# A three-block model on one core: the decay of the gated linear attention computed beside its product, a bias table written in eight parts, constants on another queue

## The chip, the core and the metric

One Trainium2 chip, one of its cores. The metric is the device time of one launch in microseconds. All arithmetic is fp32; the products are made of three passes over operands that are split into a high part (fp32r) and a low part.

## What is computed

Three transformer-like blocks over 512 tokens of 1024 features (528 in block 1, with 16 meta tokens). Block 1: RWKV-7 mixing and differential attention, gates, an MLP. Block 2: a gated convolution and sparse attention with a relative-position bias. Block 3: mLSTM, gated linear attention (GLA) and gated delta net, then gates and an MLP. The change touches three places of it.

```
h = rms_norm(h_res, norm_mix_w)                      # block 1, opening
p = h @ w_in ;  r,k,v,w,a,g from p, token shift       # block 1, projections
bias(h, distance) = rel_bias[bucket(distance), h]     # block 2, table of 8 x 640 values

q, k, v, gate, low = split(h3 @ w_in_3)               # block 3, GLA
log_decay = log_sigmoid(low @ w_gla_lr + b_gla) / 16
for each token t:  S = exp(log_decay[t]) * S + k[t] v[t]^T ;  o[t] = S^T q[t] / sqrt(128)
o = rms_norm_per_head(o) * silu(gate)

o_m = rms_norm_per_head(mlstm) * g_head_mlstm         # HeadNorm, block 3
```

## The kernel before, in words

Every engine has its own program and its own order, written out by hand; semaphores tie them together. A `stage` is a block of five such programs, with a barrier of all engines at its end, which also frees the stage's memory and semaphores.

*`opening`* (L1898) normalises x for block 1 and makes the tables of the bias. SP's queue brings x, `ones`, the norm weight and the first weight slab (L1922 to L1926), writes the row of 640 biases of each head 128 times to DRAM (`bias_by_distance`, called `far`, L1928: 2560 KB from 8 partitions) and a table by residue (`near`, L1930), and waits for both. ScalarE squares x, copies the rows out of PSUM, takes the root (L1962), issues the loads of twelve constants (L1964), and then rounds the eight normalised tiles to their high parts (L1967); VectorE multiplies (L1991) and makes the low parts (L1988).

*`rwkv_project`* (L569) multiplies h with 27 weight slabs of 512 KB in a ring of three (`first` and two `wbuf`). Its eight rounds each make r, k, v, decay, a and gate for two heads. SP's program of a round (L627 to L634): the three slabs of the round after next, a wait for `fac_ready` (VectorE's last operation of the round, `bonus`) and `g_out`, three stores (`factors`, `bonus`, `gate`), then the vectors of two rounds on. ScalarE (L744 to L767) in a round: two sigmoids, a square, one eviction and the high part of a slab that SP has just ordered, the gate's copy, three exponentials, the root `kn`, two more evictions and high parts. VectorE (L779 to L822) makes the factors; POOL makes the slabs' low parts (L646). The stage ends when all stores have landed.

*`chain`* (L97) is the product over a list of jobs, used throughout. A slab s is 8 k-tiles of one output tile: 24 matmuls. With ring=3, ScalarE makes the high part of slab s+2 in its step s (L249), VectorE its low part (L331), and evicts tile s (L381), which waits for the product of slab s. TensorE waits for the low part of each slab (L220). A `side` object can add operations of its own at each step, on each engine, behind the chain's (L239, L319, L449). Its matmuls go to one of the two `stat` banks. In block 3 the first `chain` makes 2 small tiles and the 16 tiles of z (q 0 to 3, k 4 to 7, v 8 to 11, gate 12 to 15) with `GateRows` (L2296) at its side: the gate rows of mLSTM and delta net, in steps 1 to 6.

*`gla`* (L2480) follows: SP loads the low-rank gate weight and bias, TensorE multiplies (L2541), VectorE adds the bias (L2692), ScalarE takes Abs, Exp and Ln, VectorE makes the log decay (L2697, L2698), its running sums `cum` in windows of 128 (L2700), the distance to the window's end in `ring[2]` (L2703), ScalarE its exponential (L2634), VectorE multiplies it into the keys (L2706), and only then can TensorE transpose these keys (L2560) and make the states (L2566, L2734 to L2736). In between the values are transposed and copied (L2550, L2632). Seven levels of scores inside a window follow; POOL makes the arguments of three of them (L2527).

*`HeadNorm`* (L1467) stands at the side of block 3's last `chain`. For head h in steps 3h to 3h+2: ScalarE squares o_m (L1492) behind its eviction, TensorE sums over the partitions (L1483), VectorE and ScalarE make the root (L1503, L1495), VectorE the reciprocal and the product (L1506, L1510).

Of the kernel before, what the change touches and what calls it, by code (L numbers as in the profile page):

```python
# [9 lines left out]
ALU = mybir.AluOpType  # L10
ACT = mybir.ActivationFunctionType
AX_X = mybir.AxisListType.X
P = 128
# [547 lines left out]
T2 = 512  # L561
# [7 lines left out]
def rwkv_project(nc, c, w, first, h, fac_scr, chunk_decay, bonus_scr, gate_scr):  # L569
# [5 lines left out]
    with stage(nc) as s:  # L575
# [14 lines left out]
            s.sem(n) for n in ("hi_ready", "lo_ready", "w_used", "evicted", "cleared", "mu_in", "mixed", "low_ready"))  # L590
        loaded, stored = ([s.sem(n) for _ in range(2)] for n in ("loaded", "stored"))
# [14 lines left out]
        with nc.Block() as block:  # L606
            @block.sync
            def _(sp):
# [16 lines left out]
                for i in range(8):  # L625
# [841 lines left out]
class HeadNorm:  # L1467
# [11 lines left out]
    def pe(self, pe, s, stat):  # L1479
        self.stat = stat  # L1480
        if s < 12 and s % 3 == 0:
            pe.wait_ge(self.sq_ready, s // 3 + 1)
            self.nc.tensor.matmul(stat[0][:], self.ones[:], self.sq[:], start=True, stop=True).then_inc(self.summed, 1)  # L1483

    def act(self, act, s):
# [7 lines left out]
        elif s < 12 and s % 3 == 1:  # L1493
# [3 lines left out]
    def dve(self, dve, s):  # L1497
        h = s // 3
        if s < 12 and s % 3 == 1:
# [4 lines left out]
        elif s < 12 and s % 3 == 2:  # L1504
# [393 lines left out]
def opening(nc, a, c, both, x, h, far, near, first):  # L1898
# [3 lines left out]
    W = far.shape[2]  # L1902
    M = near.shape[1] * near.shape[2]
    names = CONSTANTS[0][2:3] + CONSTANTS[0][1:2] + CONSTANTS[1]
    with stage(nc) as s:
        w, sq, rstd = s.sb("norm_w", [P, 8]), s.sb("squares", [P, 8, T1]), s.sb("rstd", [P, T1])
        rb, rev, res = s.sb("rb", [33, 8]), s.sb("rev", [33, W]), s.sb("res", [33, M])
        row, cmp_row = s.sb("row", [8, W]), s.sb("cmp_row", [8, M])
        acc, ps_r, ps_c = (s.ps(n, [P, 2, BANK]) for n in ("sum_squares", "ps_r", "ps_c"))
        x_in = [s.sem("x_in") for _ in range(8)]  # L1910
        ones_in, w_in, tables_in, first_in, const_in, filled, rows_ready, row_out, cmp_out, stored, squared, order, summed, mean_ready, root_ready = (
            s.sem(n) for n in ("ones_in", "w_in", "tables_in", "first_in", "const_in", "filled", "rows_ready", "row_out", "cmp_out", "stored",
# [5 lines left out]
        with nc.Block() as block:  # L1918
            @block.sync
            def _(sp):  # L1920
# [6 lines left out]
                sp.wait_ge(row_out, 1)  # L1927
                sp.dma_start(far, row[:].rearrange("h (a w) -> h a w", a=1).broadcast_to([8, P, W])).then_inc(stored, 16)  # L1928
# [3 lines left out]
                sp.wait_ge(stored, 32)  # L1932
# [16 lines left out]
            def _(act):  # L1949
# [8 lines left out]
                copy(row[:].rearrange("h (a w) -> h a w", a=2), ps_r[0:8, :, 0:W // 2], ACT.Copy).then_inc(row_out, 1)  # L1958
# [4 lines left out]
                for name in names:  # L1963
                    act.dma_start(c[name][:], a[name]).then_inc(const_in, 16)  # L1964
# [3 lines left out]
                act.wait_ge(const_in, 16 * len(names))  # L1968
# [327 lines left out]
class GateRows:  # L2296


    def __init__(self, nc, c, small, rows):
        self.nc, self.c, self.small, self.rows = nc, c, small, rows  # L2300

    def prepare(self, s_, evicted_d):
        self.evicted_d = evicted_d
        self.raw, self.ax, self.lin = s_.sb("raw", [4, 4, T2]), s_.sb("ax", [4, 2, T2]), s_.sb("lin", [4, 2, T2])
        self.fwd, self.end, self.ea = s_.sb("cum", [4, T2]), s_.sb("end", [4, T2]), s_.sb("ea", [4, 1])
# [6 lines left out]
    def act(self, act, s):  # L2312
# [5 lines left out]
        elif s == 3:  # L2318
            act.wait_ge(self.x_ready, 2)
            copy(ax[:], lin[:], ACT.Abs).then_inc(self.ln_ready, 1)  # L2320
            act.wait_ge(self.ln_ready, 1)
            copy(ax[:], ax[:], ACT.Exp, scale=-1.0).then_inc(self.ln_ready, 1)
            act.wait_ge(self.ln_ready, 2)
            copy(ax[:], ax[:], ACT.Ln, bias=1.0)
            copy(self.ea[:], self.c["gate_bias"][:, 3:4], ACT.Exp)
            copy(rows[:, 5, :], self.raw[:, 2, :], ACT.Sigmoid).then_inc(self.ln_ready, 1)
        elif s == 5:
# [3 lines left out]
            copy(rows[:, 7, :], self.end[:], ACT.Exp)  # L2331

    def dve(self, dve, s):
# [8 lines left out]
        elif s == 4:  # L2342
# [4 lines left out]
            seq(scan(fwd[:], c["ones"][0:4, 0:1].broadcast_to([4, T2]), lin[:, 0, :], 0.0, ALU.mult, ALU.add))  # L2347
            seq(STT(out=rows[:, 0, :], in0=raw[:, 0, :], scalar=b[:, 0:1], in1=fwd[:], op0=ALU.add, op1=ALU.subtract))
            seq(scan(rows[:, 1, :], rows[:, 0, :], rows[:, 0, :], 0.0, ALU.max, ALU.max))
            seq(STT(out=rows[:, 2, :], in0=fwd[:], scalar=-1.0, in1=rows[:, 1, :], op0=ALU.mult, op1=ALU.subtract))  # L2350
# [1214 lines left out]
```

## Time and profile before

| what | value |
|---|---|
| median of 3 runs | 3821.92 us (3819.36 to 3830.99) |
| profiled execution | 3828.68 us, span 3826.9 us |
| granted TensorE clock, mean | 0.922 of full speed |
| PE busy | 3395.8 us (89%) |
| VectorE busy | 2032.3 us (53%) |
| ScalarE busy | 1235.7 us (32%) |
| POOL busy | 214.0 us (6%) |
| 16 DMA engines, queue 1 (SP) | 268.71 MB, 21.9% |
| 16 DMA engines, queue 10 (ScalarE) | 15.47 MB, 1.6% |

The span runs from the first to the last instruction of the profiled execution; its own time has 1.8 us around it. Shares are averages over stages with different limits: in most of the program TensorE is the bound, in the stretches that the change touches it often is not. The stretches before: opening 0 to 75.9 us, projections to 308.9, the product with GateRows 2565 to 2681, `gla` to 2786, the start of the last chain from 3180.

### The profile page before, as it was taken

To read this page: it belongs to the slowest core of one execution; us is meant where nothing else is said; L and a number is where in the kernel's file an instruction comes from. 1 tells how busy PE (TensorE), PEld (TensorE's weight loads), DVE (VectorE), ACT (ScalarE), POOL (GpSimd) and SP (SyncE) were. 2 spreads that over 40 slices of the span, in tenths; PEclk is the share of its full clock that TensorE was granted. 3 is DMA by queue.
4 is the path that set the end of the run, shared out by engine and by line. 5 is a ranking of instruction groups with operands and counts; after the bars stand their busy time and mean duration, and the time that the engine had idled before them with its cause. 6 is when DMAs were issued, how large, how long until landed. Compare 5 with 4: busy or idle time off the path is not lost. (4 is left out here: it accounts for less than half of the span.)

```text
span 3826.9 us, 57163 instructions
## 1 busy us (share of the span) xinstructions
PE 3395.8 (89%) x24046; PEld 2776.4 (73%) x24046; DVE 2032.3 (53%) x3290; ACT 1235.7 (32%) x2144; POOL 214.0 (6%) x187
## 2 busy tenths in 40 slices
PE   2996899988999999989999998969499698999998
PEld 1986888955888887757777777857378386878886
DVE  2885564555355344676546775354646445465342
ACT  2552233345333233223333222232422324333231
POOL 1321220010000000000000000000100120000000
PEclk9997898988999999975799999989699689999999
DMA  5332112201222322610122223322022002232221
GB/s 114 119 140 68 46 32 91 88 1 39 94 93 94 99 94 69 172 35 12 45 78 88 88 88 94 93 65 72 2 88 91 0 2 83 77 106 95 97 99 56
DMA packets 99340, 287.81 MB, mean 75 GB/s; under 512 B 19618, under 2 KB 23842, under 8 KB 97040
## 3 DMA queue, kind: packets, MB, share of 16 engines
q1 hardware_dynamic: 92456, 268.71, 21.9%
q10 hardware_dynamic: 6632, 15.47, 1.6%
q8 instruction: 191, 3.13, 0.3%
q14 instruction: 61, 0.50, 0.0%
HBM read 264.22 MB, written 19.89 MB: 74 GB/s over the span
## 5 line engine op out<-in xcount | busy, mean ns | idle before, releaser
L233 PE MATMUL acc<-h_hi,whi 128*128 128x512 f32 x1992 | 800.9, 402 | 74.4 <-DVE wlo L425 50.2
L233 PE MATMUL acc<-h_hi,wlo 128*128 128x512 f32 x1992 | 791.6, 397 | 0.0
L233 PE MATMUL acc<-h_lo,whi 128*128 128x512 f32 x1928 | 769.9, 399 | 0.0
L233 PEld LDWEIGHTS acc<-h_hi,whi 128*128 128x128 f32 x1992 | 379.1, 190 | 184.2 <-DVE wlo L425 52.6
L331 DVE TENSOR_TENSOR wlo<-wbuf,whi 128x1024 fp32r<-128x1024 f32 (+3 forms) x277 | 318.6, 1150 | 268.6 <-ACT whi L249 266.0
L233 PEld LDWEIGHTS acc<-h_hi,wlo 128*128 128x128 f32 x1992 | 379.4, 190 | 87.8
L233 PEld LDWEIGHTS acc<-h_lo,whi 128*128 128x128 f32 x1928 | 367.0, 190 | 86.9 <-issue 3.1
L249 ACT ACTIVATE whi<-wbuf 128x1024 fp32r<-128x1024 f32 (+3 forms) x277 | 274.5, 991 | 358.5 <-PE acc L233 335.3
L233 PE MATMUL acc<-arena_round,whi 128*128 128x512 f32 x736 | 236.9, 393 | 4.8 <-DVE arena_round L391 4.8
L331 DVE TENSOR_TENSOR wlo<-ahead,whi 128x1024 fp32r<-128x1024 f32 (+3 forms) x132 | 152.3, 1154 | 137.0 <-ACT whi L249 136.3
L249 ACT ACTIVATE whi<-ahead 128x1024 fp32r<-128x1024 f32 (+3 forms) x132 | 131.4, 996 | 178.6 <-PE acc L233 173.1
L658 PE MATMUL acc<-h_hi,whi 128*128 128x264 f32 x432 | 127.9, 296 | 65.2 <-POOL wlo L646 65.2
L233 PEld LDWEIGHTS acc<-arena_round,whi 128*128 128x128 f32 x736 | 139.4, 190 | 34.9 <-DVE arena_round L391 5.7
L233 PE MATMUL acc<-arena_round,wlo 128*128 128x512 f32 x416 | 162.9, 392 | 0.0
L233 PE MATMUL acc<-gates_round,whi 128*128 128x512 f32 x384 | 141.2, 395 | 3.0 <-DVE gates_round L391 1.8
L397 DVE TENSOR_TENSOR x<-acc,x 128x512 f32<-128x512 f32 x64 | 44.3, 692 | 178.4 <-PE acc L233 178.4
L658 PEld LDWEIGHTS acc<-h_hi,whi 128*128 128x128 f32 x432 | 83.0, 192 | 69.1 <-POOL wlo L646 65.9
L233 PE MATMUL acc<-gates_round,wlo 128*128 128x512 f32 x320 | 125.5, 392 | 0.0
L658 PE MATMUL acc<-h_lo,whi 128*128 128x264 f32 x432 | 123.9, 287 | 0.0
L658 PE MATMUL acc<-h_hi,wlo 128*128 128x264 f32 x432 | 123.9, 287 | 0.0
L1415 PE MATMUL acc<-h_hi,whi 128*128 128x264 f32 x384 | 115.9, 302 | 1.2 <-DVE wlo L1453 1.2
L282 ACT ACTIVATE val<-tmp 128x512 f32<-128x512 f32 x64 | 40.5, 632 | 216.7 <-DVE tmp L393 216.7
(730 smaller groups left out, 6365.6 us busy)
## 6 DMA issues: line engine op xcount, KB each, us to landing
wbuf<-in_mlp_out SPq DMA_DIRECT2D x46, 512.0 KB, 3.3
wbuf<-in_mlp_in SPq DMA_DIRECT2D x45, 512.0 KB, 3.3
wbuf<-in_w_gates SPq DMA_DIRECT2D x38, 512.0 KB, 3.4
wbuf<-in_ffn_up SPq DMA_DIRECT2D x29, 512.0 KB, 3.4
wbuf<-in_w_qkv SPq DMA_DIRECT2D x23, 512.0 KB, 3.6
rwkv_factors<-factors SPq DMA_DIRECT2D x8, 1320.0 KB, 4.6
f<-rwkv_factors SPq DMA_DIRECT2D x8, 1280.0 KB, 6.7
ahead<-in_mlp_in SPq DMA_DIRECT2D x19, 512.0 KB
```

What stands on the lines that cost most here:

```text
L233: mm = nc.tensor.matmul(acc[t % NB][:, 0:T], wt[s % ring][:, k - a, :], xt, start=(kx == 0 and q == 0), stop=(kx == job.K - 1 and q == 2))
L249: copy(whi[s % ring][:, 0:size(s), :], wbuf[s % ring][:, 0:size(s), :], ACT.Copy).then_inc(hi_ready, 1)
L282: copy(val[t % 2][:], tmp[t % 2][:], ACT.Square)
L331: TT(wlo[s % ring][:, 0:size(s), :], wbuf[s % ring][:, 0:size(s), :], whi[s % ring][:, 0:size(s), :].bitcast(F32), ALU.subtract).then_inc( ...
L397: TT(job.dst[n], ps, job.other[n], ALU.add).then_inc(evicted_d, 1)
L658: mm = nc.tensor.matmul(acc[n % 2][:, hf, 0:H], wt[n % R][:, kx, :], xt[:, kx, at], start=(kx == 0 and q == 0), stop=(kx == 7 and q == 2))
L1415: mm = nc.tensor.matmul(acc[n % NB][:, h, 0:H], wt[n % R][:, k, :], xt[:, k, h * H:(h + 1) * H], start=(k == 0 and q == 0), stop=(k == 7 a ...
```

## The change

Four parts.

1. `opening`: the twelve constants are loaded by SP, behind the first slab and ahead of the residue table, and no longer by ScalarE; the wait for them at the end is SP's. The write of `far` is gone from it; its source `row` becomes a buffer that lives through the next stage.
2. `rwkv_project`: in each of the eight rounds SP writes 16 of the 128 copies of the row (320 KB), behind the round's three stores and ahead of the vectors and the next slabs. The stage waits for all eight at its end.
3. `GlaGates`, a new side object, takes the gates' product, log decay, running sums, far argument, its exponential and the decayed keys out of `gla` and puts them into steps 6 to 16 of the product that makes z; `Both` runs it behind `GateRows`. Buffers `cum`, `far`, `dec` are allocated outside the two stages; the log decay stands in `o_l`, the logarithm in z[12:16] until those tiles are written, and GateRows' buffers move into z as well. `gla` keeps the rest.
4. `HeadNorm`: TensorE's sum is issued in step 3h+1 instead of 3h, and the operations behind it one step later each.

```diff
-def rwkv_project(nc, c, w, first, h, fac_scr, chunk_decay, bonus_scr, gate_scr):
+def rwkv_project(nc, c, w, first, row, far, h, fac_scr, chunk_decay, bonus_scr, gate_scr):
...
                     sp.dma_start(gate_scr[:, i, :], gates[i % 2][:]).then_inc(stored[i % 2], 16)
+                    sp.dma_start(far[:, 16 * i:16 * i + 16, :], row[:].rearrange("h (a w) -> h a w", a=1).broadcast_to([8, 16, 640])).then_inc(far_out, 16)
                     if i + 2 < 8:
                         vectors(i + 2)
...
+                sp.wait_ge(far_out, 16 * 8)
...
-        if s < 12 and s % 3 == 0:
+        if s < 12 and s % 3 == 1:
             pe.wait_ge(self.sq_ready, s // 3 + 1)
             self.nc.tensor.matmul(stat[0][:], self.ones[:], self.sq[:], start=True, stop=True).then_inc(self.summed, 1)
...
-                sp.wait_ge(row_out, 1)
-                sp.dma_start(far, row[:].rearrange("h (a w) -> h a w", a=1).broadcast_to([8, P, W])).then_inc(stored, 16)
+                for name in names:
+                    sp.dma_start(c[name][:], a[name]).then_inc(const_in, 16)
                 sp.wait_ge(cmp_out, 1)
                 sp.dma_start(near, cmp_row[:].rearrange("h (a c) -> h a c", a=16)).then_inc(stored, 16)
                 sp.wait_ge(first_in, 16)
-                sp.wait_ge(stored, 32)
+                sp.wait_ge(const_in, 16 * len(names))
+                sp.wait_ge(stored, 16)
...
-                for name in names:
-                    act.dma_start(c[name][:], a[name]).then_inc(const_in, 16)
...
+class GlaGates:
...
+    def pe(self, pe, s, stat):
+        self.stat = stat
+        if s in (6, 8):
+            if s == 6:
+                pe.wait_ge(self.w_in, 32)
+                pe.wait_ge(self.evicted_d, 2)
+            else:
+                pe.wait_ge(self.lin_ready, 2)
+            for q in range(2):
+                h = s - 6 + q
+                mm = self.nc.tensor.matmul(stat[q][:], self.wl[:, h * P:(h + 1) * P], self.lr, start=True, stop=True)
+            mm.then_inc(self.x_ready, 1)
+
+    def act(self, act, s):
+        copy, pos = self.nc.scalar.activation, self.pos
+        if s == 2:
+            act.dma_start(self.wl[:], self.c["gla_w"]).then_inc(self.w_in, 16)
+            act.dma_start(self.bl[:], self.c["gla_b"]).then_inc(self.w_in, 16)
+        elif s == 9:
+            act.wait_ge(self.lin_ready, 4)
+            copy(pos, self.lin, ACT.Abs).then_inc(self.abs_ready, 1)
+            act.wait_ge(self.abs_ready, 1)
+            copy(pos, pos, ACT.Exp, scale=-1.0).then_inc(self.pow_ready, 1)
+        elif s == 10:
+            act.wait_ge(self.pow_ready, 1)
+            copy(pos, pos, ACT.Ln, bias=1.0).then_inc(self.ln_ready, 1)
+        elif s == 14:
+            act.wait_ge(self.far_arg, 1)
+            copy(self.far[:], self.far[:], ACT.Exp).then_inc(self.far_exp, 1)
+            copy(self.dec[:], self.cum[:].rearrange("p h (n t) -> p h n t", t=GW)[:, :, :, GW - 1], ACT.Exp)
+
+    def dve(self, dve, s):
...
+        if s in (7, 9):
+            dve.wait_ge(self.x_ready, (s - 5) // 2)
+            for q in range(2):
+                h = s - 7 + q
+                TS(lin[:, h, :], self.stat[q][:], self.bl[:, h:h + 1], None, ALU.add).then_inc(self.lin_ready, 1)
+        elif s == 8:
+            dve.wait_ge(self.evicted_d, 6)
+            TS(z[:, 0:4, :], z[:, 0:4, :], K_SCALE, None, ALU.mult)
+        elif s == 11:
+            dve.wait_ge(self.ln_ready, 1)
+            STT(out=lin, in0=lin, scalar=0.0, in1=self.pos, op0=ALU.min, op1=ALU.subtract).then_inc(self.steps, 1)
+            dve.wait_ge(self.steps, 1)
+            TS(lin, lin, 1.0 / 16, None, ALU.mult).then_inc(self.steps, 1)
+        elif s in (12, 13):
+            dve.wait_ge(self.steps, 2)
+            for h in range(2 * (s - 12), 2 * (s - 12) + 2):
+                scan(cum[:, h, :], self.c["chunk_start128"][:], lin[:, h, :], 0.0, ALU.mult, ALU.add).then_inc(self.cum_ready, 1)
+        elif s == 14:
+            dve.wait_ge(self.cum_ready, 4)
+            bw, fw = (ap[:].rearrange("p h (n t) -> p (h n) t", t=GW) for ap in (cum, far))
+            TT(fw, bw[:, :, GW - 1:GW].broadcast_to([P, 4 * GNW, GW]), bw, ALU.subtract).then_inc(self.far_arg, 1)
+        elif s == 16:
+            dve.wait_ge(self.far_exp, 1)
+            dve.wait_ge(self.evicted_d, 10)
+            TT(far[:], far[:], z[:, 4:8, :], ALU.mult)
...
-        wl, bl, w = s.sb("wl", [16, 512]), s.sb("bl", [P, 4]), s.sb("w", [P, 4])
-        lin, cum = s.sb("lin", [P, 4, T2]), s.sb("cum", [P, 4, T2])
-        ring = [s.sb("ring", [P, 4, T2]) for _ in range(3)]
+        w = s.sb("w", [P, 4])
+        ring = [s.sb("ring", [P, 4, T2]) for _ in range(2)] + [far]
+        kt = s.sb("kt", [P, 12, P])
```

On SP in the projections, from one round's `gate` store to the next round's vectors (all DMAs of one queue), before:

```order
L632 DMA rwkv_gate<-gate 128x528
L615 DMA vec<-in_rwkv_vec 128x8
L616 DMA lora_w<-in_lora_up 128x384
L612 DMA first<-in_w_rwkv 128x1024
L612 DMA wbuf<-in_w_rwkv 128x1024 x2
L630 DMA rwkv_factors<-factors 128x2640
L631 DMA rwkv_bonus<-bonus 128x528
L632 DMA rwkv_gate<-gate 128x528
```

and in the change:

```order
L633 DMA rwkv_gate<-gate 128x528
L634 DMA bias_by_distance<-row 8x16x640
L616 DMA vec<-in_rwkv_vec 128x8
L617 DMA lora_w<-in_lora_up 128x384
L613 DMA first<-in_w_rwkv 128x1024
L613 DMA wbuf<-in_w_rwkv 128x1024 x2
L631 DMA rwkv_factors<-factors 128x2640
L632 DMA rwkv_bonus<-bonus 128x528
L633 DMA rwkv_gate<-gate 128x528
```

One DMA of 8 x 16 rows of 640 values has come between the stores and everything that is loaded behind them, once a round.

On VectorE in the product that makes z, steps 9 to 13 (`wlo` is a low part, `z<-acc` an eviction, `o_l_plain` holds the gates and then the log decay), the change has:

```order
L331 TENSOR_TENSOR wlo<-wbuf,whi 128x1024
L381 TENSOR_TENSOR z<-acc,scale 128x512
L2417 TENSOR_SCALAR o_l_plain<-stat,bl 128x512 x2
L331 TENSOR_TENSOR wlo<-ahead,whi 128x1024
L381 TENSOR_TENSOR z<-acc,scale 128x512
L331 TENSOR_TENSOR wlo<-wbuf,whi 128x1024
L381 TENSOR_TENSOR z<-acc,scale 128x512
L2423 SCALAR_TENSOR_TENSOR o_l_plain<-o_l_plain,z 128x2048
L2425 TENSOR_SCALAR o_l_plain<-o_l_plain 128x2048
L331 TENSOR_TENSOR wlo<-wbuf,whi 128x1024
L381 TENSOR_TENSOR z<-acc,scale 128x512
```

Before, the same steps held only the low parts and the evictions, two to a step; the operations on `o_l_plain` stood in `gla`.

## Rows read from the trace of the kernel before

**Rows 1.** Timeline, opening: start us, us, engine, line, operation xcount [idle before <-releaser].

```profile
15.50 4.72 ACTq L1964 DMA_DIRECT2D ident<-in_ident  x1
...
19.26 1.45 DVE L1991 SCALAR_TENSOR_TENSOR squares<-x,norm_w,rstd 128x528 f32<-128x528 f32 x2
...
64.98 1.18 ACT L1967 ACTIVATE h_hi<-squares 128x528 fp32r<-128x528 f32 x2 [49.24 <-issue]
...
75.95 1.06 ACT L723 ACTIVATE whi<-first 128x1024 fp32r<-128x1024 f32 x1 [1.74 <-PEq L42]
```

**Rows 2.** DMA, 16 to 30 us: queues (packets, MB, share); issues (KB, us to landing).

```profile
q1 hardware_dynamic: 271, 0.69, 47.6%
q10 hardware_dynamic: 216, 0.08, 2.2%
...
chunk_start<-in_chunk_start ACTq DMA_DIRECT2D x1, 264.0 KB, 15.7
...
bias_by_distance<-row SPq DMA_DIRECT2D x1, 2560.0 KB
...
rwkv_factors<-factors SPq DMA_DIRECT2D x8, 1320.0 KB, 4.6
```

**Rows 3.** Timeline of SP, one round of the projections.

```profile
236.58 0.33 SPq L630 DMA_DIRECT2D rwkv_factors<-factors  x1
...
241.36 0.33 SPq L612 DMA_DIRECT2D first<-in_w_rwkv  x1
```

**Rows 4.** Timeline of ScalarE and VectorE, the same round.

```profile
246.07 1.06 ACT L723 ACTIVATE whi<-first 128x1024 fp32r<-128x1024 f32 x1 [1.60 <-DMA first<-in_w_rwkv]
...
251.97 0.61 ACT L764 ACTIVATE kn<-zb 128x528 f32<-128x528 f32 x1
...
252.61 0.43 DVE L813 TENSOR_SCALAR kn<-kn 128x528 f32<-128x528 f32 x1 [0.99 <-ACT kn L764]
...
259.41 0.71 DVE L821 TENSOR_TENSOR bonus<-za,factors 128x528 f32<-128x528 f32 x1
```

**Rows 5.** Waits, 135 to 262 us: total us, times, longest.

```profile
ACT whi L723 <- DMA first<-in_w_rwkv: 6.9, 5, 2.5
...
DVE kn L813 <- ACT kn L764: 4.1, 5, 1.0
```

**Rows 6.** Timeline, end of the projections.

```profile
302.62 0.93 SPq L632 DMA_DIRECT2D rwkv_gate<-gate  x1
308.95 0.77 DVE L1181 MEMSET f<- 128x240 f32 x3 [7.20 <-PEq L42]
```

**Rows 7.** Timelines of POOL, PE, ScalarE and VectorE in `gla`.

```profile
2681.69 1.80 POOL L2678 MEMSET scores<- 128x2048 f32 x1 [1801.46 <-POOLq L42]
...
2691.34 1.11 PE L2550 MATMUL psT<-ident,z 128*128 128x128 f32 x4
...
2717.51 1.06 ACT L2640 ACTIVATE ring<-ring 128x1024 f32<-128x1024 f32 x1 [3.66 <-DVE ring L2527]
...
2727.86 0.35 DVE L2736 SCALAR_TENSOR_TENSOR z<-z,dec,psX 128x128 f32<-128x128 f32 x1
```

**Rows 8.** The product before `gla` and the durations moved into it: timelines, line L211, waits.

```profile
2624.34 0.69 DVE L381 TENSOR_TENSOR z<-acc,scale 128x512 f32<-128x512 f32 x1 [3.29 <-PE acc L233]
...
2629.92 0.69 DVE L381 TENSOR_TENSOR z<-acc,scale 128x512 f32<-128x512 f32 x1 [3.09 <-PE acc L233]
...
2701.31 2.29 DVE L2697 SCALAR_TENSOR_TENSOR lin<-lin,ring 128x2048 f32<-128x2048 f32 x1 [5.88 <-ACT ring L2629]
2703.64 1.23 DVE L2698 TENSOR_SCALAR lin<-lin 128x2048 f32<-128x2048 f32 x1
...
L211 PE MATMUL stat<-sums,ones x4: 592/592/593, 1539.6 to 2575.6; 128*128 128x512 f32 x4
...
PE acc L233 <- DVE wlo L331: 5.7, 3, 4.3
```

**Rows 9.** Waits, 3175 to 3290 us (the last chain's start).

```profile
PE stat L1483 <- ACT sums L1492: 10.1, 4, 3.0
```

More of the change, by code:

```diff
@@ L1895, in dve, with opening @@
                 TT(self.a[:, i, :], self.a[:, i, :], self.rstd[:], ALU.mult).then_inc(self.norm_ready, 1)
-def opening(nc, a, c, both, x, h, far, near, first):
+def opening(nc, a, c, both, x, h, row, near, first):
     H = T1 // 2
-    W = far.shape[2]
+    W = row.shape[1]
     M = near.shape[1] * near.shape[2]
@@ L2330, in act @@
             act.wait_ge(self.end_ready, 1)
-            copy(rows[:, 7, :], self.end[:], ACT.Exp)
+            copy(rows[:, 7, :], self.end, ACT.Exp).then_inc(self.exp_done, 1)
     def dve(self, dve, s):
@@ new lines, with __init__, prepare, pe @@
+class Both:
+    def __init__(self, first, second):
+        self.first, self.second = first, second
+    def prepare(self, s_, evicted_d):
+        self.first.prepare(s_, evicted_d)
+        self.second.prepare(s_, evicted_d)
+    def pe(self, pe, s, stat):
+        self.first.pe(pe, s, stat)
+        self.second.pe(pe, s, stat)
+    def act(self, act, s):
+        self.first.act(act, s)
+        self.second.act(act, s)
+    def dve(self, dve, s):
+        self.first.dve(dve, s)
+        self.second.dve(dve, s)
@@ L2477, with gla @@
 SMALL = 32
-def gla(nc, c, z, lr, o, weight, diags):
+def gla(nc, c, z, o, weight, diags, cum, far, dec):
     NB = 4 * GNW
@@ L2623, in _ @@
                 copy = nc.scalar.activation
-                act.wait_ge(lin_ready, 1)
-                copy(ring[0][:], lin[:], ACT.Abs).then_inc(abs_ready, 1)
-                act.wait_ge(abs_ready, 1)
-                copy(ring[0][:], ring[0][:], ACT.Exp, scale=-1.0).then_inc(pow_ready, 1)
-                act.wait_ge(pow_ready, 1)
-                copy(ring[0][:], ring[0][:], ACT.Ln, bias=1.0).then_inc(ln_ready, 1)
                 for h in range(4):
@@ L2632, in _ @@
                     copy(vt[:, GNW * h:GNW * (h + 1), :].rearrange("p n d -> p (n d)"), psT[(h + 1) % 2][:], ACT.Copy).then_inc(v_copied, 1)
-                act.wait_ge(far_arg, 1)
-                copy(ring[2][:], ring[2][:], ACT.Exp).then_inc(far_exp, 1)
-                copy(dec[:], cum[:].rearrange("p h (n t) -> p h n t", t=GW)[:, :, :, GW - 1], ACT.Exp).then_inc(dec_ready, 1)
                 def level(li):
@@ L3244, in first_block @@
                 first = resident(nc, m3, "first", [P, 8, P])
-                opening(nc, a, c, both, x, h, far, near, first)
-                rwkv_project(nc, c, a["w_rwkv_1"], first, h, factors, decay, bonus, gate)
+                row = resident(nc, m3, "row", [8, 640])
+                opening(nc, a, c, both, x, h, row, near, first)
+                rwkv_project(nc, c, a["w_rwkv_1"], first, row, far, h, factors, decay, bonus, gate)
             rwkv_tiles(nc, c, y, factors, decay)
```

96 lines of the change are left out of this document (38 added, 58 removed).

## The prediction

> **What bounds the kernel now.** Four stretches are touched, and each has its own limit, so the page's shares of busy time (PE 89%) say little. I read them in the order of the program.
>
> *The opening* [rows 1]. In the timeline the reader should look for what ScalarE does between 15 and 65 us: nothing but issuing twelve loads of constants at over 4 us each. The first `h_hi` cast stands behind them on ScalarE and starts at 64.98, though its input was ready at 20.0, when VectorE's first product (19.26 + 0.73) ended. Nothing else in the core worked. Why an issue took 4.7 us is in the DMA rows [rows 2]: SP's write of 2560 KB of `bias_by_distance` was under way. From 16 to 30 us its queue moved 271 packets in 47.6% of 16 engines' time: 0.476 x 16 x 14.0 / 271 = 0.39 us a packet of 2560 bytes, 49 GB/s in all.
>
> *The projections* [rows 3 to 5]. Round i ends when VectorE finishes the bonus; SP then stores three arrays and, behind them, loads the next weights. In the round shown: stores from 236.58, load of `first` issued 241.36, ScalarE casts it at 246.07 after waiting 1.60 us for that very load, ends `kn` at 252.58, VectorE, which waited 0.99 us for it, ends the bonus at 260.12. So 236.58 to 260.12 is a closed ring: store, load, cast, exponentials, reciprocal, store. There are five rounds in which ScalarE waits for the load (6.9 us in all) and VectorE waits for `kn` in as many. These waits are short, but they are above zero: a later load is a later round.
>
> *The gated attention stage `gla`* [rows 7]. It takes 46.5 us from the memset at 2681.69 to the end of the states at 2728.21; most of this is one dependent chain on VectorE and ScalarE with TensorE idle. *The product before it* runs at TensorE's pace once past its first slabs: one slab each 5.58 us [rows 8]. *The last long product* [rows 9]: TensorE waited four times, 10.1 us in all, for the square of HeadNorm.
>
> **The change part by part.**
>
> *Opening, constants to SP, far write out: -44.7 us.* ScalarE has no DMA left behind the root. Its first cast starts at 20.0 in place of 64.98. The work behind it keeps its pace (75.95 - 64.98 = 11.0 us before; VectorE had two products ready then, which I count as 0.2 us): the next stage starts near 31.2 instead of 75.95. The twelve loads, some 1.6 MB, now follow 2.7 MB of `x` and weights on SP's queue; at the rate of a store of all partitions (1320 KB in 4.6 us [rows 2]) they need 6 us, and even at half that rate they land by 25 us, with the 31 KB of `bias_by_residue` right behind: under the casts. If that cover is short by 5 us, 5 us are lost.
>
> *Eight parts of the far write in the projections: +36.3 us.* Each part is 1/8 of 2560 KB: 128 packets. It stands behind the stores and ahead of `vec`, `lora_w` and the three weights on SP's queue. At the rate of rows 2 a part takes 320 x 1024 / 52e9 = 6.3 us (52 GB/s being 2560 bytes x 8 / 0.39 us, the share of one half read as eight engines busy). The load of `first` moves back by that, less a little because the other engines run ahead: I take 6.0. Parts 0 to 4 each stand before a load that ScalarE waits for, hence 5 x 6.0 = 30. Parts 5 and 6 stand only before vectors that are wanted 15 us later: nothing. Part 7 stands at the stage's end, where the last stores [rows 6] (issued 302.62) hold the next stage until 308.95: 6.3 more. TensorE stays covered: its work fits into a round now and gets 6 us more room. Bounds of one part: 0 (the queue overlaps it with loads) and 15.7 us, what a constant took to land beside these writes [rows 2].
>
> The Trainium skill (page "DMA: Bandwidth & Descriptors", section "Rules for kernel authors") says that an outermost dimension of size c under 16 confines a DMA to c engines, and this DMA's is 8; the share of 47.6% agrees. Its Specifications give about 27 GiB/s for an engine, by which a part would be 1.4 us, the whole term 8.4 instead of 36.3 and the time 3749; the trace shows 6.6 GB/s an engine on these packets, and the measurement decides.
>
> *`gla`: -31 us.* Gates, logarithm, scans, the far argument, its exponential and the decayed keys are gone from it. What is left before the end of the states: four groups of value transposes (1.11 us a group [rows 7]) and the copy behind the last, about 5 us, then what ran from the level-0 exponential at 2717.51 to 2728.21, 10.7 us. That is 15.7 against 46.5: -31. What follows in the stage is unchanged and bound by VectorE.
>
> *The product that takes these steps in: +4.7 us.* TensorE gets four matmuls of 16 rows, 8 instructions at 592 ns (the nearest full-clock rows [rows 8]) = 4.7 us; this is all that lies on its path. VectorE gets 17 us in steps 7 to 16 of 5.58 us each, of which low part and eviction take 1.9. The fullest is step 11 (2.29 + 1.23 [rows 8] + 1.9 = 5.4). ScalarE gets Abs and Exp at step 9 behind a wait for a gate that VectorE can add only after slab 9: that releases it some 6.2 us after slab 9, and the high part of slab 12, then the low part, end 8.4 us after it; TensorE wants them at 11.2. At step 14 the far exponential holds ScalarE till about 34 us after slab 9, low part 17 is done at 36.5, wanted at 39. So cost nothing, by margins of 2.5 us and more. GateRows' memory in z and its one more wait cost nothing: those tiles of z are written from step 8 on. The two loads at ScalarE's step 2 are issued before a wait of 2.4 us that was there.
>
> *HeadNorm one step later: -10.1 us.* The sum now stands after slab 3h+1, some 5 us after its square is made. The four waits go; the four matmuls stay. The later VectorE and ScalarE pieces move by a slab each and end at step 12, long before `o_m` is used.
>
> *Sum:* -44.7 + 36.3 - 31 + 4.7 - 10.1 = **-44.8 us**. From the profiled execution's 3828.68 that is 3783.9. That execution stands 6.8 us above the median of 3821.92, so for the median: **3777.1**.
>
> **Rivals.**
>
> A, *the parts are cheap.* The factors' store moved 1320 KB in 4.6 us [rows 2], about 18 GB/s an engine; at that rate on eight engines a part is 2.2 us, and six of them 13.4 instead of 36.3: 3754.2. For it: the eight engines' slowness may come from a megabyte-long backlog. Against it: the 0.39 us held from 16 to 30 us with an almost empty second queue. Were parts wholly hidden, 3741.
>
> B, *slower: the parts stall the weights much longer.* If a part delays the load behind it as long as the constants were delayed, 15.7 us, the projections gain 6 x 15.7 = 94 us against 81.1 saved elsewhere: 3835. It decides above 13.5 us a part. Against it: then two queues took turns packet by packet, and several DMAs stood in line; here one queue with 16 packets an engine.
>
> C, *the moved steps stall their product.* GateRows shows the way: with ScalarE held in its steps, TensorE waited 5.7 us in three times for a low part [rows 8]. Two such stalls of 5.7 in steps 9 to 15 would give 3788.5. For it: ScalarE blocks in program order, and margins rest on my adding up. Against: 2.5 us of margin and a ring of three.
>
> D is that constants or the residue row land late in the opening; it costs 5 us and lies within the forecast's own width.
>
> **How the numbers follow.** Forecast 0.67, own range 3767 to 3789 (5.0 to 7.5 us a part, 29 to 33 for `gla`). A 0.15, C 0.15, B 0.03. For 8 in 10 I go from 3745, half way into A's hidden end, to 3793, past C. A measurement of this kernel tells 0.3% (11.5 us) from no change: faster 0.95, same 0.02, slower 0.03.
>
> **What would show it.** Opening: ScalarE's first cast near 20 us, next stage near 31. Projections: ScalarE's wait for `first` at about 7.5 us in five rounds, rounds of 29.5 us, VectorE's wait for `kn` grown by 6. `gla`: states end 16 us after the memset. Its product: TensorE waits for nothing after slab 6, four matmuls more. Last product: no wait at the HeadNorm sum. If the rounds stay at 23.6 us, the step on the parts is wrong; if the product before `gla` grows by 10 us, the step on margins is.

## The result and the profile after

| | before | changed |
|---|---|---|
| median of the runs, us | 3822.6 (4 runs) | 3778.75 (4 runs, 3769.33 to 3783.06) |
| profiled execution, us | 3828.68 | 3783.06 |
| its span, us | 3826.9 | 3781.2 |

The kernel before was run once more beside the change, hence 3822.6 for 3821.92. The ratio is 0.9878, with a 95% interval of 0.9857 to 0.9898: the change is faster by 1.2%, 43.9 us between the medians and 45.6 between the profiled executions (3828.68 - 3783.06). The prediction was 3777.1 and a difference of -44.8. The median came 1.7 us above the forecast and the difference 0.9 us short of it, yet four of the five terms were off by 2 to 7 us, in both directions.

Page of the changed kernel, part 1 (busy time, share) and part 3 (queues: packets, MB, share):

```profile
PE 3394.1 (90%) x24046; PEld 2778.2 (73%) x24046; DVE 2022.4 (53%) x3290; ACT 1234.1 (33%) x2144; POOL 210.5 (6%) x187
...
q1 hardware_dynamic: 94064, 270.35, 22.2%
q10 hardware_dynamic: 5080, 13.83, 1.4%
```

**The opening** (timeline of the changed kernel, to be laid beside [rows 1]):

```profile
6.34 0.43 SPq L1932 DMA_DIRECT2D norms<-in_norms  x1
...
11.59 0.43 SPq L1932 DMA_DIRECT2D rope_swap<-in_rope_swap  x1
...
20.09 1.32 ACT L1970 ACTIVATE h_hi<-squares 128x528 fp32r<-128x528 f32 x2 [4.33 <-DVE squares L1993]
...
31.05 1.06 ACT L726 ACTIVATE whi<-first 128x1024 fp32r<-128x1024 f32 x1 [1.72 <-PEq L42]
```

SP issues the constants in 0.43 us each where ScalarE took over 4. The first `h_hi` cast stands at 20.09, released by VectorE, and the next stage starts at 31.05 for 75.95: -44.9.

**One round of the projections**, the one that answers to [rows 3, 4] (timelines of SP, ScalarE, VectorE and POOL):

```profile
220.40 0.33 SPq L631 DMA_DIRECT2D rwkv_factors<-factors  x1
...
222.19 1.29 SPq L634 DMA_DIRECT2D bias_by_distance<-row  x1
...
224.82 2.90 SPq L617 DMA_DIRECT2D lora_w<-in_lora_up  x1
227.76 3.72 SPq L613 DMA_DIRECT2D first<-in_w_rwkv  x1
...
234.80 1.06 ACT L726 ACTIVATE whi<-first 128x1024 fp32r<-128x1024 f32 x1 [4.99 <-DMA first<-in_w_rwkv]
...
246.02 2.34 POOL L649 TENSOR_TENSOR wlo<-wbuf,whi 128x1024 fp32r<-128x1024 f32 x1 [0.81 <-ACT whi L726]
...
246.04 2.88 DVE L820 SCALAR_TENSOR_TENSOR factors<-kn,eprev 128x528 f32<-128x528 f32 x1
...
251.05 0.33 SPq L631 DMA_DIRECT2D rwkv_factors<-factors  x1
```

The round takes 251.05 - 220.40 = 30.65 us, 7 more than before (260.15 - 236.58 = 23.57). From store to cast it is 14.4 us, before 9.5: the part stands between them, and SP itself is held 2.90 and 3.72 us in issuing the loads behind it. From cast to next store it is 16.25 us, before 14.1; the 2.2 us more are in one row, VectorE's `factors<-kn,eprev`. It takes 2.88 us for the usual 0.71: it starts 0.02 us behind GpSimd's low part and ends 0.56 us after it (248.92 and 248.36).

The whole stage goes from 233.0 us (75.95 to 308.95) to 276.7 (31.05 to 307.77): +43.7. Its waits, 50 to 280 us, and its end (timeline) answer to [rows 5, 6]:

```profile
PE za L674 <- issue: 36.8, 6, 7.6
...
ACT whi L726 <- DMA first<-in_w_rwkv: 28.0, 5, 6.7
```

VectorE's waits, 90 to 256 us (before, 135 to 262 us, its wait for `eneg` was 5.3 us in two times):

```profile
DVE factors L811 <- ACT eneg L763: 45.6, 5, 10.5
DVE kn L816 <- ACT kn L767: 4.9, 5, 1.0
```

The end of the stage:

```profile
296.06 1.29 SPq L634 DMA_DIRECT2D bias_by_distance<-row  x1
...
307.77 0.77 DVE L1184 MEMSET f<- 128x240 f32 x3 [13.53 <-PEq L42]
```

**Stage `gla`**, which answers to [rows 7] (timelines of POOL, VectorE, TensorE and ScalarE, and the next stage's first cast):

```profile
2682.26 1.81 POOL L2753 MEMSET scores<- 128x2048 f32 x1 [1805.47 <-POOLq L42]
...
2682.30 2.29 DVE L2624 TENSOR_TENSOR ring<-cum 128x2048 f32<-128x2048 f32 x1 [1.03 <-PEq L42]
2682.30 1.07 PE L2638 MATMUL psT<-ident,z 128*128 128x128 f32 x8 [1.76 <-PEq L42]
...
2684.32 1.09 ACT L2710 ACTIVATE vt<-psT 128x512 f32<-128x512 f32 x2 [0.26 <-PE psT L2638]
...
2685.30 1.06 ACT L2715 ACTIVATE ring<-ring 128x1024 f32<-128x1024 f32 x1
...
2694.29 0.35 DVE L2793 SCALAR_TENSOR_TENSOR z<-z,dec,psX 128x128 f32<-128x128 f32 x1
...
2753.59 1.34 ACT L296 ACTIVATE whi<-ahead 128x256 fp32r<-128x256 f32 x4 [10.18 <-PEq L42]
```

From memset to the end of the states it is 12.4 us (before 46.5), and to the next stage's cast 71.3 us (before 105.8, its cast at 2787.44): -34.4. The value transposes before, and here (windows as below: us, busy time by engine, granted clock, DMA share, GB/s):

```profile
2690.00:2694.00 4.00, 2.45 (x6) 0.71 (x4) 2.55 (x4) 0.00 (x0) 0.00 (x0) 0.50 0.00 0
```

```profile
2682.00:2685.00 3.00, 2.25 (x17) 1.74 (x17) 2.29 (x1) 1.77 (x4) 2.74 (x2) 1.00 0.02 1
```

**The product before it**, which answers to [rows 8]: TensorE's waits from 2563 to 2682 us, the low part of the slab whose cast stands behind GlaGates' Abs and Exp, and the matmuls of GlaGates (the first four in the timeline, then all eight).

```profile
PE acc L233 <- DVE wlo L331: 3.7, 3, 2.4
...
2642.67 1.23 DVE L331 TENSOR_TENSOR wlo<-ahead,whi 128x1024 fp32r<-128x1024 f32 x1 [4.88 <-ACT whi L249]
...
2609.45 1.98 PE L2388 MATMUL stat<-small,wl 16*128 16x512 f32 x4
...
L2388 PE MATMUL stat<-small,wl x8: 587/587/692, 2609.5 to 2629.4; 16*128 16x512 f32 x8
```

From its first cast to the memset of `gla` the product takes 118.3 us (2563.95 to 2682.26), before 115.6 (2566.06 to 2681.69): +2.7. TensorE's last wait is the one of 2.4 us ahead of slab 7, at 2613.86, where it had been 4.3; after 2616 us it waits nowhere.

**The last long product.** The wait of [rows 9] for the square is gone. The same 388 matmuls, in the kernel before and then in the changed one (windows: us, busy time of PE, PEld, DVE, ACT, POOL, TensorE's granted clock, DMA share, GB/s):

```profile
3180.70:3287.00 106.30, 95.86 (x388) 74.68 (x389) 52.39 (x51) 44.84 (x55) 0.00 (x0) 0.97 0.31 104
```

```profile
3148.20:3241.70 93.50, 93.10 (x388) 74.06 (x389) 52.61 (x51) 44.90 (x55) 0.00 (x0) 0.98 0.36 118
```

-12.8 us: TensorE is idle 0.4 us and not 10.4, and its work takes 2.8 us less. Its clock stood at the lower level for two intervals of 3.4 us in the first stretch and for one in the second; one interval fewer is worth 1.7 us, an estimate from half of 3.4, and the other 1.1 us are open.

Together -44.9 + 43.7 + 2.7 - 34.4 - 12.8 = -45.7, where the spans differ by 45.7. The code between these places is the same in both kernels and drifted up to 8 us apart on the way, with under 1 us of it left at the end.

### The profile page after: what moved, and what is told of

It reads as the page before. It is cut to its first block and busy times, and to the rows that moved or that the text cites. A ratio compares the mean times of both kernels' runs of the same rounds, so it can differ in the third digit from the quotient of the medians.

```text
span 3781.2 us, 57168 instructions
## 1 busy us (share of the span) xinstructions
PE 3394.1 (90%) x24046; PEld 2778.2 (73%) x24046; DVE 2022.4 (53%) x3290; ACT 1234.1 (33%) x2144; POOL 210.5 (6%) x187
## 5 line engine op out<-in xcount | busy, mean ns | idle before, releaser
L233 PEld LDWEIGHTS acc<-h_hi,whi 128*128 128x128 f32 x1992 | 379.0, 190 | 184.2 <-DVE wlo L425 53.7
L661 PE MATMUL acc<-h_hi,whi 128*128 128x264 f32 x432 | 129.8, 300 | 20.2 <-POOL wlo L649 20.2
L661 PE MATMUL acc<-h_lo,whi 128*128 128x264 f32 x432 | 125.3, 290 | 0.0
L1418 PE MATMUL acc<-h_lo,whi 128*128 128x264 f32 x384 | 109.7, 286 | 0.0
```

The source lines that it names most:

```text
L233: mm = nc.tensor.matmul(acc[t % NB][:, 0:T], wt[s % ring][:, k - a, :], xt, start=(kx == 0 and q == 0), stop=(kx == job.K - 1 and q == 2))
L661: mm = nc.tensor.matmul(acc[n % 2][:, hf, 0:H], wt[n % R][:, kx, :], xt[:, kx, at], start=(kx == 0 and q == 0), stop=(kx == 7 and q == 2))
L1418: mm = nc.tensor.matmul(acc[n % NB][:, h, 0:H], wt[n % R][:, k, :], xt[:, k, h * H:(h + 1) * H], start=(k == 0 and q == 0), stop=(k == 7 a ...
```

## The experiments

The open question was the largest loss, +43.7 us in the projections. Is it the place of the parts on SP's queue, or that they are written beside this stage at all? And why is the write slow? All times are medians; ratios are to the kernel before on the same chip, where that kernel's own median lay between 3822.2 and 3825.5, so two or three microseconds between kernels of different sets of runs say nothing.

**The place of the parts.** The same DMA, issued behind the round's weight loads:

```
                     for n in group(i + 2):
                         weight(n)
+                    sp.dma_start(far[:, 16 * i:16 * i + 16, :], row[:].rearrange("h (a w) -> h a w", a=1).broadcast_to([8, 16, 640])).then_inc(far_out, 16)
                     sp.wait_ge(fac_ready, i + 1)
...
                     sp.dma_start(gate_scr[:, i, :], gates[i % 2][:]).then_inc(stored[i % 2], 16)
-                    sp.dma_start(far[:, 16 * i:16 * i + 16, :], row[:].rearrange("h (a w) -> h a w", a=1).broadcast_to([8, 16, 640])).then_inc(far_out, 16)
```

> The eight parts of bias_by_distance are issued behind each round's three weight loads and not ahead of them. Theory Q (a part costs because the loads of vec, lora_w and first stand behind it on SP's queue): the load of first lands as early as in the kernel before, rounds go back from 30.7-32.0 us to 23.6, the stage's end from 13.5 us of waiting to 7.2, the projections from 276.7 to 233 us, and the time is 3778.75 - 43.7 = 3735. Rival W (a part costs wherever it stands, since it takes eight engines from the weights and its writes slow the stores): the projections stay above 260 us and the time above 3762. The half-speed intervals of TensorE's clock in the rounds, five here and one before, go under Q and stay under W.

Measured: **3734.22 us**, ratio 0.9765 (0.9736 to 0.9794), 44.5 us below the change. Rounds of 23.2 to 24.8 us; the projections take 233.4 us. Waits, 50 to 235 us, and the stage's end (timeline):

```profile
ACT whi L726 <- DMA first<-in_w_rwkv: 6.3, 4, 2.5
```

```profile
264.45 0.77 DVE L1184 MEMSET f<- 128x240 f32 x3 [7.20 <-PEq L42]
```

Theory Q. All of the loss was the order on one queue; the parts themselves cost nothing that shows (233.4 us with them, 233.0 in the kernel before without). Of the five half-speed intervals in the rounds two remain, of 3.4 us each; before the change there was one.

**The parts twice.** Each part again, to a scratch tensor, right behind the first:

> Each part is written twice, the second time to a scratch tensor. If its cost is its own transfer on the queue, each of the five rounds and the stage's end grow by 6.3 to 7.3 us again, and rounds 5 and 6 stay nearly covered: +38 to +46, time 3817 to 3825. Rival: what costs is a fixed delay behind the first part (an issue that blocks, the collision of GpSimd's low part with VectorE): under +20, time below 3799.

Measured: 3817.94 us, ratio 0.9984 (0.9972 to 0.9996), +39 on the change. The five rounds grew by 6.6, 4.4, 6.7, 6.4 and 6.7 us, round 5 by 1.2, round 6 by nothing, the last wait from 13.5 to 20.2: 6.2 us a round for the second part. From the store to the cast all five grew alike, by 6.5 to 6.9 us, about the 6.6 us that a part's packets take; the second grew less in all because no VectorE operation stands beside GpSimd's low part on its ring any more (cast to store 14.1 us for 16.1). ScalarE's wait for `first`:

```profile
ACT whi L728 <- DMA first<-in_w_rwkv: 58.0, 5, 13.1
```

**The parts on ScalarE's queue**, and off SP's.

```
                     copy(hv(kn[:]), zb[:, :, 0:H], ACT.Sqrt).then_inc(root_ready, 1)
+                    act.dma_start(far[:, 16 * i:16 * i + 16, :], row[:].rearrange("h (a w) -> h a w", a=1).broadcast_to([8, 16, 640])).then_inc(far_out, 16)
```

> Each part is issued on ScalarE's queue right behind the root of its round, some 8 us before SP's stores. Theory Q: SP's queue is free for the weights, the part is done before the stores; what is left is ScalarE's time of issue, 8 x 0.5 us at most: 3735 to 3740. Rival: the issue blocks ScalarE as the constants' did in the opening of the kernel before (4.7 us each), behind which the evictions and casts of the round wait: five rounds longer by 3 to 5 us, 3750 to 3760.

Measured: 3740.36 us, ratio 0.9774 (0.9751 to 0.9796), projections 233.3 us. The issue is short (timeline of ScalarE), so the rival falls:

```profile
179.92 0.27 ACTq L767 DMA_DIRECT2D bias_by_distance<-row  x1
```

**The load of `first` before the stores.** The converse test: the parts stay where the change has them, and the load that is waited for is taken out from behind them.

```
-                for n in range(R, 9):
+                for n in range(R, 10):
                     weight(n)
                 for i in range(8):
-                    for n in group(i + 2):
+                    for n in range(3 * i + 10, min(3 * i + 13, NT)):
                         weight(n)
```

> The change with its parts where they are, ahead of two weight loads, but with the load of first issued one place earlier, before the round's stores. Theory Q (a part costs only because the load of first, for which ScalarE waits, stands behind it): ScalarE's wait for first (28.0 us in five rounds) goes, the parts are hidden in the rounds, and the stage's end alone keeps its 6.3 us: 3778.75 - 36.4 - 1.6 = 3741, down to 3734 if the waits that were there before the change go too. Rival: the next load, of wbuf, then holds ScalarE: rounds of 26 us and more, time above 3750.

Measured: 3740.01 us, ratio 0.978 (0.9764 to 0.9796). ScalarE's wait for `first` is no longer in the list, its largest being for TensorE, and the five rounds are 23.2 us each. Only the end keeps its part, 6.3 us, which is why this is 39 us below the change and not 44. ScalarE's waits, 50 to 250 us, and the end (timeline):

```profile
ACT rkv L734 <- PE acc L661: 64.8, 22, 6.1
```

```profile
266.18 0.77 DVE L1184 MEMSET f<- 128x240 f32 x3 [13.54 <-PEq L42]
```

**Both moves together.**

> The parts behind the weights, as in e2_parts_behind_weights, and the load of first before the stores. ScalarE waited 6.3 us in four rounds for first there. If that load closed the ring, rounds of 24.0 to 24.8 us come down by 1.3 to 2.5 us and the time is 3727. Rival: another ring (ScalarE's own work and its waits for TensorE) sets the round once the load is early: 3731 to 3734, no change from 3734.22 that can be measured.

Measured: **3729.68 us**, ratio 0.9758 (0.9741 to 0.9775). Rounds of 23.2 us again, end wait 7.2, projections 228.5 us for 233.4. In the trace each of the five rounds is up to 1.6 us shorter than with the first move alone, 4.8 us in the stage; between the medians it is 4.5 us, which the ranges of the two (3723 to 3744 and 3723 to 3736) do not separate. It is the fastest median of the study.

**What makes the write slow.** The row is stored in DRAM once and the parts are written from there: with the 16 copies outermost, and, in the second kernel, with the 8 heads outermost as in the change.

```
+                sp.dma_start(row_scr, row[:]).then_inc(row_out, 16)
...
-                    sp.dma_start(far[:, 16 * i:16 * i + 16, :], row[:].rearrange("h (a w) -> h a w", a=1).broadcast_to([8, 16, 640])).then_inc(far_out, 16)
+                    if i == 0:
+                        sp.wait_ge(row_out, 16)
+                    sp.dma_start(far[:, 16 * i:16 * i + 16, :].rearrange("h a w -> a h w"), row_scr.rearrange("h (a w) -> a h w", a=1).broadcast_to([16, 8, 640])).then_inc(far_out, 16)
```

> The same bytes and the same place, but the row is first stored in DRAM, and a part is written from there with the 16 copies as its outermost dimension and the 8 heads inside. If a part's 6.3 us come from eight engines with 0.39 us a packet, sixteen engines need 3.1 us: projections +22 instead of +43.7, time 3757. If the source of eight partitions also made the packets slow, and from DRAM they take the 0.14 us of a store (18 GB/s an engine), a part is 1.1 us and the time 3742. Rival: the number of engines has no part in it (the writes to DRAM or their 2560-byte packets set it): 3779 again.

> As e3_parts_wide, from the stored row in DRAM, but with the 8 heads outermost and the 16 copies inside, as in the change: eight engines again. In the change a packet of 2560 bytes took 392 ns, in e3_parts_wide 102 ns. Theory S (the eight partitions as a source make the packets slow): they take 102 ns again, a part 16 x 0.10 = 1.6 us, and the time is within 8 us of e3_parts_wide's 3744.5. Rival N (the eight engines do it): the packets take 392 ns, and the time is 3779.

Measured: 3744.51 (ratio 0.9788, 0.9769 to 0.9807) and 3743.57 us (0.9789, 0.9773 to 0.9805). The DMA view within a part of the last round (packets, MB, share of 16 engines), for the change over 4.0 us, for the row from DRAM with 8 heads outermost over 1.5 us, and with 16 copies outermost over 1.2 us:

```profile
q1 hardware_dynamic: 75, 0.19, 46.2%
```

```profile
q1 hardware_dynamic: 115, 0.27, 49.5%
```

```profile
q1 hardware_dynamic: 178, 0.39, 97.8%
```

Share x 16 x window / packets is the time of one packet: 0.394, 0.103 and 0.105 us. The shares of one half with 8 outermost and of nearly all with 16 go with the number of engines that the outermost dimension sets. But what made a packet slow was its source: from DRAM the same 2560 bytes take 0.10 us on eight engines as on sixteen. In the kernel with the parts behind the weights, where a part starts while weights of the same queue are still under way, the same `row` came to 0.154 us a packet (1.5 us of its fourth part; 61 of these 65 packets are the row's, the others have 4 bytes):

```profile
q1 hardware_dynamic: 65, 0.16, 41.7%
```

Packet by packet, in the trace's records of single packets, `row`'s took 0.10, 0.2 or 0.39 us there: 0.13 us on average where no more than about four of them were under way (101 packets), 0.31 where nearly eight were (574), and 0.39 in the change, where nearly eight almost always were (917). So its partitions are not slow of themselves; they are slow when many engines read them at once. Why some of eight at once were still fast in the mixed case is not shown. The 128 packets of a part in the change took 6.6 us, 50 GB/s.

The Trainium skill has a rule that fits (page "SBUF — State Buffer", section "Door 1: The DMA port swizzle"): four neighbouring partitions share a DMA port, and there are 16 ports for 435 GB/s. By it `row`'s eight partitions reach two ports, an estimate of 54 GB/s; the trace's 50 agrees. No run moved `row` to other partitions, so that it is the ports stays argued.

Neither kernel gained the full 43.7 us: the parts still stood ahead of `first`, and 320 KB took its share (first round 27.8 us, then 24.7 to 25.5, in the one; 24.5 to 28.0 in the other; end waits of 8.6 and 9.4).

**The same cure in the opening.** If the source was the trouble, the opening of the kernel before needs no move at all. First the kernel *before* with this edit alone, constants still on ScalarE:

```
-                sp.dma_start(far, row[:].rearrange("h (a w) -> h a w", a=1).broadcast_to([8, P, W])).then_inc(stored, 16)
+                sp.dma_start(row_scr, row[:]).then_inc(row_stored, 16)
+                sp.wait_ge(row_stored, 16)
+                sp.dma_start(far.rearrange("h a w -> a h w"), row_scr.rearrange("h (a w) -> a h w", a=1).broadcast_to([P, 8, W])).then_inc(stored, 16)
```

> The kernel before with one edit: the row is stored in DRAM and the whole write of bias_by_distance in the opening comes from there, copies outermost, over sixteen engines. Theory S (the opening was held by a write whose source is eight partitions): 2560 KB at the 324 GB/s of e3_parts_wide take 8 us and not over 50, the constants behind the root are issued in under 1 us each, the first h_hi cast stands at 21 to 27 us instead of 65 and the next stage at 32 to 38 instead of 76: 3822 - 41 = 3781, within 4 us. Rival V (a write of 2560 KB fills the queues from whatever source, and ScalarE's issues stay at 4 us and more): less than half of the 44.9 us comes back, time above 3800.

Measured: **3778.89 us**, ratio 0.9877 (0.9856 to 0.9898), the time of the whole change. Timeline of ScalarE and DMA view of 16 to 30 us (KB, us to landing):

```profile
16.88 0.52 ACTq L1967 DMA_DIRECT2D mean<-in_mean  x1
...
22.47 1.18 ACT L1970 ACTIVATE h_hi<-squares 128x528 fp32r<-128x528 f32 x2 [6.36 <-issue]
...
33.45 1.06 ACT L723 ACTIVATE whi<-first 128x1024 fp32r<-128x1024 f32 x1 [1.75 <-PEq L42]
```

```profile
chunk_start<-in_chunk_start ACTq DMA_DIRECT2D x1, 264.0 KB, 8.4
```

This edit changed two things at once, the source and the outermost dimension (128 copies and not 8 heads). Which of them was needed here no run separates; the pair of kernels above says that the source alone brings a packet down to 0.10 us.

Then the change without parts, the whole write in its opening, and `first` before the stores:

> The change with no parts in the projections: the write stands whole in the opening behind bias_by_residue, from the row in DRAM, and the load of first is issued before the stores as in e11_both_moves. Theory S: the write runs from some 17 to 27 us under the casts, the next stage starts at 31 to 33 us, rounds are 23.2 us, the stage's last wait is 7.2 us, and the time is that of e11_both_moves, 3730, up to 3733. Rival: the opening's end waits for the write, 5 us and more: above 3735.

Measured: 3733.36 us (3719.1 to 3734.43), ratio 0.9752 (0.973 to 0.9774). The next stage starts at 30.81 us, the projections take 228.2. The trace has the same rounds as with both moves, 23.2 us, so the parts there were hidden entirely; their medians, 3729.68 and 3733.36, are not apart by more than either spreads.

**Which half freed the opening?** The change, with the constants behind ScalarE's root again:

```
                 copy(rstd[:], rstd[:], ACT.Sqrt).then_inc(root_ready, 1)
+                for name in names:
+                    act.dma_start(c[name][:], a[name]).then_inc(const_in, 16)
```

> The twelve constants are issued by ScalarE behind the root again, as before the change; the far write stays out of the opening. Theory F (their 4.7 us each came from the far write's megabytes under way): an issue takes some 0.45 us, the first h_hi cast stands 12 x 0.45 = 5.4 us later, and the time is 3784. Rival I (a load issued there by ScalarE is slow of itself): the cast is at 65 us again and the time 3823.

Measured: 3782.69 us, ratio 0.9891 (0.9875 to 0.9907). Timeline of ScalarE:

```profile
15.49 0.36 ACTq L1966 DMA_DIRECT2D norms<-in_norms  x1
...
20.71 0.45 ACTq L1966 DMA_DIRECT2D rope_swap<-in_rope_swap  x1
21.21 1.18 ACT L1969 ACTIVATE h_hi<-squares 128x528 fp32r<-128x528 f32 x2 [5.09 <-DVE squares L1993]
```

Theory F, at a lower price: twelve issues of 0.45 us fit into the wait for VectorE, and the cast moves 1.1 us and not 5.4. The -44.9 us came from taking the write out; moving the constants is worth 1 us of it (next stage at 32.17 for 31.05; the medians, 3.9 us apart, can't tell so little).

**GlaGates alone undone.**

> The change with GlaGates alone undone: gates, logarithm, scans, far argument and decayed keys stand in gla again; GateRows keeps its place in z. From the traces: the stage and its tail were 34.4 us shorter, the product before it 2.4 us longer, so +32: 3811. By the terms of the prediction (-31 and +4.7) it is +26: 3805. Rival: part of the 34.4 us came from TensorE's clock in that execution alone: under +22, below 3800.

Measured: 3809.3 us, ratio 0.996 (0.9946 to 0.9973), +30.5 on the change. `gla` with its tail takes 104.2 us again (memset at 2676.11, cast at 2780.33). In the product before it TensorE waits as it did before the change:

```profile
PE acc L233 <- DVE wlo L331: 5.7, 3, 4.3
```

So GlaGates' matmuls do not only cost: its first group stands in a stretch where TensorE is about to wait for a low part, and 2.0 of those 5.7 us vanish beside it.

**HeadNorm alone undone.**

> The change with HeadNorm alone undone. From the traces +12.8 us, 10.1 of waits and the rest a half-speed interval of 3.4 us in that stretch: 3791.5, four waits for the square of 2 to 3 us each are back. By the prediction's term +10.1: 3789. Rival: the waits come back and are caught up by the ring of three slabs: within 4 us of 3779.

Measured: 3786.54 us (3770.72 to 3789.44), ratio 0.9887 (0.9866 to 0.9907), which can't be told from the change's 0.9878. The trace can tell them apart. From the chain's first cast to the same later cast of `arena_plain` it is 90.5 us in the change (3147.68 to 3238.13), 104.0 here (3140.39 to 3244.43) and 103.2 before (3180.14 to 3283.30), and the wait is back. In that stretch TensorE's clock stood at the lower level for 3.4 us once in the change, three times here and twice before.

```profile
PE stat L1486 <- ACT sums L1495: 9.4, 4, 2.6
```

## Why the prediction was right, and where its terms were off

**The opening** (-44.7, measured -44.9) was right in size and in times (cast at 20.0, stage at 31.2). Rival D, constants that land late, did not come: from 16 to 30 us SP's queue moved 4 packets. Its cause was left in two halves. The runs say: the far write alone.

**The parts** (+36.3, measured +43.7). The mechanism was right, and three runs show it: the loss goes when the part is put behind the load of `first` (3734), goes when the load is put before the part (3740), and grows by 39 us when the part is doubled. The mis-sized term is "I take 6.0" for each of five rounds: it was 36.4 / 5 = 7.3. Of the 36.4 us, 27 are delay (5.4 a round, less than the 6.3 of a part, as I had argued) and 9 are something I did not look for. The rounds shifted against GpSimd's low parts, and a VectorE operation of 0.71 us on the ring took 2.73 to 2.88 us in each of the five, where before only two were touched, by 0.3 and 1.0. The Trainium skill gives the rule (page "SBUF — State Buffer", section "SBUF: two separate sides"): a VectorE operation with two SBUF inputs and a GpSimd operation that reads SBUF lock each other out for a whole instruction. The row above, which ends 0.56 us after GpSimd's, agrees. "Parts 5 and 6: nothing" missed 1.6 us in round 5, and the stage up to its first stores was 0.6 us shorter. The last part's 6.3 at the stage's end was exact (13.53 - 7.20). One sign was named wrongly: VectorE's wait for `kn` was to grow by 6 us and stayed at 1.0 a round. The delay reached VectorE earlier in its program, in its wait for ScalarE's exponential `eneg`, 45.6 us in five times for 5.3 in two.

**Rival A** rested on "a megabyte-long backlog" as the reason of the slow packets. Parts of 128 packets had no backlog and took 0.39 us all the same. The slowness is that of the source. My forecast took the right number from [rows 2] without knowing why, and so could not say that it was avoidable. **Rival B** (15.7 us a part) fell: the constants' 15.7 us were the same slow write.

**`gla`** (-31, measured -34.4). The order was right: the level-0 exponential stands on ScalarE right behind the last copy of the values, while its argument from VectorE was ready at 2684.59. Two sizes were off. "About 5 us" up to the exponential was 3.0: the 1.11 us a group came from a row at a granted clock of 0.50, and in the changed kernel TensorE came out of the product at 1.00 and made the first two groups in 1.07 us. And from the exponential to the end of the states it took 9.3 us, not 10.7: the keys are decayed already, and their transposes start at 2684.97, 0.3 us ahead of the exponential, where before they started 2.2 us behind it (2719.73 and 2717.51). That the 1.4 us come from this start and not in part from the clock, 0.50 there at first, is not shown apart.

**The product that takes the steps in** (+4.7, measured +2.7). The step that was off is "8 instructions at 592 ns": they overlap, and a group of four takes 1.98 us, 4.0 in all. The first group stands ahead of slab 7, whose wait for its low part shrank by 1.9 us, so up to slab 7 the product is only 0.2 us longer; this was not seen. The second group costs its 2.0 us (slab 8 to slab 9 in 7.58 us for 5.58), and the slabs behind it are 0.03 us longer each, for which no run gives the reason. The margins held: behind slab 7 TensorE waits for nothing, and rival C has no stall. The nearest low part, slab 12's, was done at 2643.9, and TensorE took it at 2646.8: 2.9 us, forecast 2.8 (11.2 - 8.4).

**HeadNorm** (-10.1, measured -12.8). The waits went as said. The term counted idle time alone; TensorE's work in the stretch also took 2.8 us less, with one interval at the lower clock fewer. The term's size rests on the traces: with HeadNorm alone undone the median rose by 7.8 us, inside the spread of its own runs.

So the total was right partly by luck: +7.4 on the parts stood against -3.4, -2.0 and -2.7 elsewhere.

## What to carry to other kernels

A DMA on a queue costs what the next load behind it costs: put a write that nobody waits for behind the loads of the round, or take the load that is waited for out in front. Both hid 320 KB a round; the first gave 44 us, the second 39, since the last part still stood at the stage's end. When a write is slow, work out the time of one packet (share x 16 x window / packets) and compare it with another DMA's before scheduling around it: here a row stored once in DRAM and written from there, over sixteen engines, gave with an edit of a few lines as much as the whole change. And when a stage's rounds shift, look at which VectorE operations now stand beside GpSimd's.

## What the runs showed of the hardware

- A DMA of 2560-byte packets from eight neighbouring partitions moved 50 GB/s on eight engines; from DRAM 177 GB/s on eight and 324 on sixteen (means of the DMA views above).
- Issues beside or behind such a write are slow on both queues: 4.7 us each on ScalarE's [rows 1], 2.9 and 3.7 us on SP's; with the write from DRAM ScalarE's took 0.4 to 0.8.
- TensorE's clock followed its idle time. Over five rounds of the projections, before and after (windows):

```profile
140.50:260.20 119.70, 113.39 (x840) 107.68 (x841) 107.02 (x121) 67.02 (x86) 37.57 (x15) 0.99 0.42 154
```

```profile
95.00:251.10 156.10, 119.69 (x840) 112.27 (x841) 102.38 (x122) 67.99 (x87) 38.01 (x16) 0.89 0.42 129
```

The same 840 matmuls took 6.3 us more, at a granted clock of 0.89 for 0.99: in each of the five idle stretches of 6.8 to 7.6 us, one at the end of a round, it fell to its lower level, 1.2 GHz, for 6.8 to 10.2 us. Here TensorE had room: from cast to next store the five rounds took 2.0 to 2.2 us more than 14.1, and that is the excess of the one VectorE operation, so the lower clock added nothing.
